# One transformer layer with adaLN, one core: adaLN sums over the free axis, weights laid out in blocks, and five k-passes in the first feed-forward stage

## What is computed

```python
cond = jax.nn.silu(c)                       # 2048 values
mod = cond @ w_ada[l] + b_ada[l]            # 2048 x 18432, nine vectors of 2048
sh1, sc1, gt1, sh2, sc2, gt2, sh3, sc3, gt3 = split(mod, 9)
u = _modulate(_rmsnorm(h, norm1_g[l]), sh1, sc1)          # x * (1 + sc1) + sh1
h = h + 0.5 * gt1 * _swiglu(u, ffn1_w_in[l], ffn1_w_out[l])
u = _modulate(_rmsnorm(h, norm2_g[l]), sh2, sc2)
h = h + gt2 * _hybrid_mixer(u, ...)
u = _modulate(_rmsnorm(h, norm3_g[l]), sh3, sc3)
h = h + 0.5 * gt3 * _swiglu(u, ffn2_w_in[l], ffn2_w_out[l])
return _rmsnorm(h, final_g)
```

## Time and profile before

| | |
|---|---|
| median of 3 runs | 2054.93 us |
| lowest, highest | 2054.68, 3204.81 us |
| span of the profiled execution | 2052.8 us |
| its mean granted TensorE clock | 0.999 |
| TensorE busy | 99% of the span |
| VectorE, ScalarE busy | 85%, 58% |
| moved by DMA | 540.80 MB, mean 263 GB/s |

### The profile page before, as it was taken

One profiled execution on the slowest core, in us unless ns is written; L12 is line 12 of the kernel. 1 busy time (PEld: TensorE's weight loads), 2 busy tenths in 40 slices (PEclk: granted clock), 3 DMA queues, 4 the chain that ended last, 5 costly groups with the idle time before them and its releaser, 6 DMA issues.

```text
span 2052.8 us, 24243 instructions
## 1 busy us (share of the span) xinstructions
PE 2030.3 (99%) x9197; PEld 1674.2 (82%) x9197; DVE 1735.4 (85%) x2038; ACT 1195.1 (58%) x1668; POOL 4.5 (0%) x22
## 2 busy tenths in 40 slices
PE   7999999999999999999999999999999999999998
PEld 6888888888888888888777888888888888888887
DVE  6998998888889898887998898988778777787786
ACT  4667444655346565446545666567775477755764
POOL 0000000000000000000000000000000000000000
PEclk9999999999999999999999999999999999999999
DMA  9998899998999778985666687565565556565554
GB/s 371 387 387 321 328 334 338 343 336 315 327 341 336 269 261 326 334 299 181 218 217 211 230 298 278 204 216 195 186 240 191 202 185 204 206 205 192 177 200 149
DMA packets 249572, 540.80 MB, mean 263 GB/s; under 512 B 11888, under 2 KB 14320, under 8 KB 248688
## 3 DMA queue, kind: packets, MB, share of 16 engines
q1 hardware_dynamic: 248368, 539.11, 74.1%
q10 hardware_dynamic: 1088, 0.15, 0.0%
HBM read 537.10 MB, written 2.11 MB: 263 GB/s over the span
## 4 chain that ended last, share of the span: by engine, by line
PE 94%; DMA 2%; DVE 2%; issue 1%; ACT 0%; SPq 0%; ACTq 0%; DVEq 0%
PE pb L909 13%; PE pb L917 13%; PE pa L909 13%; PE pb L913 13%; PE pa L917 13%; PE pa L913 12%; PE pa L1064 2%; PE pa L1058 2%; PE pa L1061 2%; DMA raw<-in_ffn_w_in_dram 1%; PE pa L1228 1%; PE pb L1219 1%; PE pb L1224 1%; PE pb L1228 1%; PE pa L1219 1%; PE pa L1224 1%
## 5 line engine op out<-in xcount | busy, mean ns | idle before, releaser
L1494 ACT CAST hi<-raw 128x1024 fp32r<-128x1024 f32 (+2 forms) x662 | 682.2, 1035 | 704.8 <-PE pb L917 316.3
L2105 DVE TENSOR_TENSOR lo<-raw,hi 128x1024 fp32r<-128x1024 f32 (+2 forms) x662 | 784.0, 1199 | 230.5 <-ACT hi L1494 228.0
L2205 DVE SCALAR_TENSOR_TENSOR ada_acc<-ada_w,cond,ada_acc 128x1024 f32<-128x1024 f32 (+1 forms) x210 | 236.7, 1127 | 6.3
L909 PE MATMUL pa<-hi,act_hi 128*128 128x512 f32 x816 | 226.4, 394 | 0.0
L909 PE MATMUL pb<-hi,act_hi 128*128 128x512 f32 x816 | 221.0, 393 | 0.0
L917 PE MATMUL pb<-lo,act_hi 128*128 128x512 f32 x816 | 218.2, 389 | 0.0
L917 PE MATMUL pa<-lo,act_hi 128*128 128x512 f32 x800 | 217.8, 389 | 0.0
L913 PE MATMUL pb<-hi,act_lo 128*128 128x512 f32 x800 | 214.0, 389 | 0.0
L913 PE MATMUL pa<-hi,act_lo 128*128 128x512 f32 x736 | 200.3, 389 | 0.0
L917 PEld LDWEIGHTS pb<-lo,act_hi 128*128 128x128 f32 x816 | 153.2, 188 | 32.0
L909 PEld LDWEIGHTS pb<-hi,act_hi 128*128 128x128 f32 x816 | 151.8, 188 | 32.7 <-issue 2.2
(11 more groups left out here) (482 smaller groups left out, 2622.1 us busy)
## 6 DMA issues: line engine op xcount, KB each, us to landing
raw<-in_ffn_w_in_dram SPq DMA_DIRECT2D x155, 1024.0 KB, 5.4
ada_w<-in_w_ada_dram SPq DMA_DIRECT2D x207, 512.0 KB, 6.4
raw<-in_w_in_dram SPq DMA_DIRECT2D x63, 1024.0 KB, 5.3
raw<-in_ffn_w_out_dram SPq DMA_DIRECT2D x60, 1024.0 KB, 5.2
ada_s<-in_w_ada_dram SPq DMA_DIRECT2D x64, 512.0 KB, 11.6
pair<-in_ffn_w_in_dram SPq DMA_DIRECT2D x20, 1024.0 KB, 6.7
raw<-in_ffn_w_out_dram SPq DMA_DIRECT2D x24, 768.0 KB, 4.5
raw<-in_w_out_dram SPq DMA_DIRECT2D x16, 1024.0 KB, 5.1
```

Of the source, the lines that this page charges most:

```text
L909: pe.matmul(bank[:, tt, cols], a_hi[:, k0 + kk, tok], w_hi[:, kk, cols], start=start and kk == 0, stop=False, skip_group_check=on)
L1494: act.copy(hi_of(ph, i, j, half)[:, 0:n, 0:w], raw_of(ph, i, j)[:, 2 * half:2 * half + n, 0:w])\
L2105: dve.tensor_tensor(lo_of(ph, i, j)[:, s, 0:w], raw_of(ph, i, j)[:, s, 0:w], hi_of(ph, i, j, half)[:, 0:n, 0:w].bitcast(F32), ALU.subtract)\
L2205: ins = dve.scalar_tensor_tensor(out=acc, in0=wt, scalar=cond[:, kt:kt + 1], in1=acc, op0=ALU.mult, op1=ALU.add)
```

## The change

**Layout.** The host now hands over every weight matrix in blocks of 512 columns, [block, partition, k-tile, column], so that a partition's part of a chunk is one run of 8 KB in memory; before it was four runs of 2 KB. The chunks of the first stage are laid out in the order of use (`w_first`). x comes token by partition, and once more transposed (`x_t`); parameters come as columns (`cols`).

**adaLN.** `w_ada` is transposed: outputs are on the partitions, k is in the free axis. TensorE spreads `cond` over all partitions once (`cond_rows`, 16 matmuls), and one instruction multiplies a tile with that row and sums it into one column of `macc` (`accum_out`). `mod_sum` adds the two halves and the bias. Folds, flushes and gate sums are gone. The modulation vector lies on the partitions at once; the gate rows, GT1's too now, are stored to DRAM in pieces of 4 bytes and loaded back over all partitions (`store_quarter`, `load_quarter`).

**First stage.** Scale and shift of one k-tile need one tile of 128 x 2048 each (1 MB), so `act_hi` exists k-tile by k-tile. `PASSES` goes through 2, 2, 4, 4 and 4 k-tiles. In a pass two column groups are done first in four double banks (`pa`, `pb`, `px`, `pq`), then the other two in the same banks; ScalarE keeps a bank in `part` and refills it from there (`keep`). `S_AT` gives the units at which VectorE sums the scale and the shift tile of each k-tile. x is not transposed on TensorE: `x_t` is multiplied with the gain and the row of 1/rms. In the opening the first scale tile is loaded between the two halves of x, and summed before the norm.

**adaLN in `ffn1_out0`.** 22 of the 24 tiles lie in its first 11 chunks.

The core of the diff:

```diff
+PASSES = ((0, 1), (2, 3), (4, 5, 6, 7), (8, 9, 10, 11), (12, 13, 14, 15))
...
-    ada_plan("ffn1_out0", [2, 1, 2, 1] * 4)
+    ada_plan("ffn1_out0", [2] * 11 + [1, 1, 0, 0, 0])
...
+    NEW = {kt: min(u for u in range(64) if kt in [b[0] for b in first_unit_of(u)[2]]) for kt in range(KD)}
+    S_AT = {0: (0, 0), 1: (1, 2), 2: (6, 7), 3: (8, 9), 4: (13, 14), 5: (16, 17), 6: (18, 19), 7: (20, 21),
+            8: (27, 28), 9: (29, 30), 10: (32, 33), 11: (34, 35), 12: (43, 44), 13: (45, 46), 14: (48, 49), 15: (50, 51)}
+    XT_PIECES = ((0, 2), (2, 4), (4, 8), (8, 16))
...
+            def store_quarter(q):
+
+                sp.wait_ge(mod_ok, mod_count(GT1, q))
+                sp.dma_start(gate_rows[0:1, q * NC:(q + 1) * NC].rearrange("a (k p) -> p (a k)", p=P),
+                             mod[:, GT1 * KD + 4 * q:GT1 * KD + 4 * q + 4], allow_slow_non_contiguous=True)\
+                    .then_inc(gt1_out, 16)
...
-            sp.dma_start(h[:, :, :], x_tok).then_inc(x_in, 16)
-            for k in range(8):
-                load_start(k)
...
+            sp.dma_start(c_in[:, :], c).then_inc(c_ok, 16)
+            for tt in range(TT):
+                sp.dma_start(h[:, tt, :], x[:, tt, :]).then_inc(x_in[tt], 16)
+                if tt == 0:
+                    load_start(0, (SC1,))
+            load_x_t(0)
+            load_start(0, (SH1,))
+            loaded = 1
+            for pos in range(32):
+                ahead = pos + (pos >= 12)
+                while loaded < KD and NEW[loaded] // 2 <= ahead:
+                    for piece, (k0, _) in enumerate(XT_PIECES):
+                        if k0 == loaded:
+                            load_x_t(piece)
+                    load_start(loaded)
+                    loaded += 1
+                load(plan["ffn1_in0"], 0, pos, w_first[pos], 4)
                 load_ada(plan["ffn1_in0"].c0 + pos)
...
+                cond_rows()
+                keep_busy(8)
+                rstd_row()
+                keep_busy(24)
+                pe.wait_ge(cond_row_ok, 4)
+                pe.wait_ge(rs_ok, 1)
+                for u in range(64):
+                    if u == 57:
+                        pe.wait_ge(pa_free, 2)
+                        transposes(0)
+                    if u in (60, 63):
+                        nb = (u - 57) // 3
+                        pe.wait_ge(nat_lo, 2 * nb)
+                        transposes(nb)
+                    first_unit(ph, u)
...
+                def keep(p, g, ab, after):
+
+                    bank = ((px, pq) if second_set(p, g) else (pa, pb))[ab]
+                    act.wait_ge(unit_used, after + 1)
+                    act.copy(part[:, g, ab, :, :], bank[:, :, :]).then_inc(part_ok if p > 0 else bank_ok, 1)
+                    if p > 0:
+
+                        other = (g + 2) % 4
+                        act.wait_ge(bank_ok, 4)
+                        act.wait_ge(part_ok, 4 * (p - 1) + 2 * (g % 2) + ab + 1)
+                        act.copy(bank[:, :, :], part[:, other, ab, :, :]).then_inc(bank_ok, 1)
...
+                for u in range(64):
+                    split(ph, 0, u // 2, u % 2, 2)
+                    for kt in range(KD):
+                        if NEW[kt] == u:
+                            first_hi(kt)
+                    for job in todo.get(u, ()):
+                        keep(*job)
...
+            def start_tile(kt, m):
+
+                k = 2 * kt + (m == SH1)
+                dve.wait_ge(ada_s_in[k % S_RING], 16 * (k // S_RING + 1))
+                wt = ada_s[:, k % S_RING, :]
+                dve.scalar_tensor_tensor(out=wt, in0=wt, scalar=1.0, in1=cond_row[:, :], op0=ALU.mult, op1=ALU.mult,
+                                         accum_out=macc[:, 0, m * KD + kt:m * KD + kt + 1]).then_inc(s_dve, 1)
...
+                for u in range(64):
+                    for kt in range(KD):
+                        if S_AT[kt][0] == u and kt > 0:
+                            start_tile(kt, SC1)
+                        if S_AT[kt][1] == u:
+                            start_tile(kt, SH1)
+                            start_mod(kt)
+                    for kt in range(KD):
+                        if NEW[kt] == u:
+                            start_lo(kt)
...
                     split(ph, 0, u // 2, u % 2, 2)
```

More of the change, by code:

```diff
@@ L123, in build, with tile_col @@
     SH1, SC1, GT1, SH2, SC2, GT2, SH3, SC3, GT3 = range(9)
[L124 to L140, removed]
+    HALF_ROWS = [(GT1, q) for q in range(4)] + [(m, half) for m in (SH2, SC2, GT2, SH3, SC3, GT3) for half in (0, 1)]
+    ROWS_OUT = (GT1, GT2, GT3)
+    ROW_TILES = [8 if m == GT1 else 16 for m, _ in HALF_ROWS]
+    TILES = [(row, sub) for row in range(len(HALF_ROWS)) for sub in range(ROW_TILES[row])]
+    def tile_col(t):
+        row, sub = TILES[t]
+        m, part_ = HALF_ROWS[row]
+        return m * KD + part_ * (ROW_TILES[row] // 2) + sub // 2, sub % 2
     n_tiles = {}
@@ L208, in s_used, with mod_after, mod_count @@
-    def s_used(q, n):
-        on_dve = sum(kt not in ON_PE[x // KD] for x in range(KD * q + n) for kt in (x % KD,))
-        return on_dve, KD * q + n - on_dve
+    MODS = [(GT1, q) for q in range(4)] + [(m, 1) for m in (SH2, SC2, GT2, SH3, SC3, GT3)]
+    def mod_after(t):
+        row, sub = TILES[t]
+        return HALF_ROWS[row] if sub == ROW_TILES[row] - 1 and HALF_ROWS[row] in MODS else None
+    def mod_count(m, part_=1):
+        return MODS.index((m, part_)) + 1
+    S_RING = 4
+    FIRST = first_chunks()
@@ L214, in build, with second_set, bank_at @@
+    def second_set(p, g):
+        return g % 2 == 1 and not (p == LAST and g == 3)
+    def bank_at(p, g, ab):
+        return 4 * p + (2 * (g - 2) if p == LAST else 2 * (g % 2)) + ab + 1
     PIECES = [(g, (0,)) for g in range(4)] + [(g, (1,)) for g in range(4)] + [(g, (0, 1)) for g in range(4, 8)]
@@ L1225, in first_unit @@
                               start=False, stop=False, skip_group_check=True)
                 pe.wait_ge(lo_done, u + 1)
-                for kk, tt, tok in places:
-                    mm = pe.matmul(bank[:, tt, :], act_hi[:, k0 + kk, tok], w_lo[:, 2 * half + kk, 0:NC],
-                                   start=False, stop=half == 1 and kk == 1, skip_group_check=True)
+                for m, tt, tok in places:
+                    mm = pe.matmul(bank(m)[:, tt, :], act_hi[:, blocks[m][0], tok], w_lo[:, s0 + m, 0:NC],
+                                   start=False, stop=True, skip_group_check=True)
@@ L1532, in in_body @@
                     split(ph, i, j, half, n)
-                    if ph is plan["ffn1_in1"] and first and n_ == 0:
-                        gate_round(3)
                     if first and mid:
@@ L2494, in body @@
                         split(ph, i, j, half, n)
-                        if name == "ffn1_in1" and first and n_ == 1:
-                            gate_rest(3)
                         if first and mid:
```

893 lines of the change are left out of this document (303 added, 590 removed).

## The result

The changed kernel takes 2068.61 us (median of 4, 2067.85 to 2071.29) where the kernel before takes 2054.84. The ratio is 1.0069, with a 95% interval of 1.0054 to 1.0084. It lies inside 2%, but the interval is clear of 1, and the time is outside the range of 2037 to 2061 that was forecast. Two single executions ran far slower (one of the kernel before, 3204.81 us; one of e11_runs_order, 2526.46 us at a granted clock of 0.752), and the ratios are taken without them.

What follows compares the result with a forecast made beforehand. TensorE, busy 99%, was taken as the bound, with VectorE next. Span 2052.8 - 0.4 (first stage) - 4.0 (rest) = 2048.4, plus 2.1 to the median, 2050.5 us; forecast's own range 2045 to 2056, 8 in 10 for 2037 to 2061.

Steps and rivals of the forecast that it cites:

- Opening: Start of the first stage: unit 0 at about 20.6 us, 15.6 us earlier than before, and unit 2 at 28.3.
- The tile: VectorE's 2048-wide scale or shift sum in the first stage: taken as 2.27 us, between 2.2 and 2.7.
- Rival C: Slower kernel because the summing tile costs more than 2.27 us; at 2.7 us, 2061.7 us in all; chance 0.15.
- Stalls (a) to (c): First stage, units 16 to 21, 28 to 35, 43 to 51: VectorE's tile bursts stall TensorE 6.3, 5.8 and 4.7 us.
- ScalarE's eight copies: Behind units 10 and 11, keeping and refilling four banks at 1.0 us a copy cuts VectorE's lead to 1.4 us.
- VectorE, not the transfers, takes it: First stage: VectorE gives back nearly all the opening's gain; the stage ends at 217.4 us against 217.75.
- rival B: Long runs bring no faster transfer: 387 GB/s instead of 417, plus 4 us, 2054.5 us; chance 0.13.
- The rest, minus 4.0: Behind the first stage: removing TensorE's gate sums saves 2.0 us and its folds 2.0 us; bounds 2.5 and 5.
- The doubled tiles: `ffn1_out0`, 22 tiles in 11 chunks: VectorE's 21.7 us per block just fits TensorE's 21.8, nothing to spare.
- The gate row "cost nothing": GT1's trip through DRAM in `ffn1_out0`: loaded some 5.4 us into the stage, some 18 us to spare, no cost.
- which sign would overturn the step: A wait of VectorE on the gate row in `ffn1_out0` or `ffn1_in1` would overturn costing it at nothing.
- the forecast's span of 2048.4: Whole kernel: the span before, 2052.8 us, less 0.4 for the first stage and 4.0 for the rest.

Runs made afterwards that it cites:

- e11_runs_order: e10_long_runs with another order in the first stage, of SyncE's tile transfers and of the units where VectorE sums them; 2039.65 us, ratio to before 0.9924.
- e3_tile_half: The changed kernel with half of each first-stage scale and shift sum left out, the transfers kept; 2061.97 us.
- e8_gate_pe_keeps: e1_gate_pe with ScalarE's first-stage bank copies spread, one pair per unit; 2056.75 us.
- e12_tile_half_both: The changed kernel with half of each first-stage scale and shift tile left out, in the sum and in the transfer; 2045.58 us.
- e13_order_again: The kernel of e11_runs_order run once more for another trace; 2040.59 us, ratio to before 0.9928.
- e10_long_runs: The changed kernel with gate rows stored in runs, 16-byte pieces for GT1 and 64-byte for GT2 and GT3; 2054.01 us, ratio to before 0.9996.
- e1_gate_pe: The changed kernel with the GT1 row spread by TensorE and copied by VectorE, instead of going through DRAM; 2056.69 us.
- e5_gate_pe_store: e1_gate_pe with the four quarter stores in 4-byte pieces kept, nothing waiting for them or reading them; 2066.88 us.
- e7_before_pieces: The kernel before with four stores of 512 4-byte pieces added, which nothing reads or waits for; 2069.69 us against 2055.29.

## Why the prediction was wrong, step by step

**Opening: right.** Unit 0 starts at 20.72 us (forecast 20.6), unit 2 at 29.00 (28.3).

**The tile: right.** A 2048-wide sum is followed after 2.21 us, with 2.27 taken. Rival C falls with it.

```profile
21.83 2.29 DVE L1995 SCALAR_TENSOR_TENSOR ada_s<-ada_s,cond_row 128x2048 f32<-128x2048 f32 x1
24.04 0.08 DVE L1995 DVE_READ_ACCUMULATOR ada_s<-ada_s,cond_row 128x1 f32 x1
```

**Stalls (a) to (c): right in place and size, the engine half right, one reason wrong.** TensorE's gaps in units 16 to 21, 28 to 35 and 43 to 51, from the start of one matmul to the next less the usual, add up to 5.2, 5.3 and 4.9 us (6.3, 5.8 and 4.7 were said). Against 2.72 us for each unit, which is how the forecast counted, the three stretches lose 6.3, 6.1 and 5.8. The stage ends at 219.5 us (217.4). They are nearly all waits for VectorE, and with half of each sum gone most of them go (e3_tile_half). But other waits, for the cast, take their place at units 34 and 50, 7.8 us of them, and only 4.8 us are won. So VectorE's bursts are one cause, and not shown to be the whole. ScalarE's eight copies, which were to cut the lead to 1.4 us, are worth 0.6 us at the stage's end (e8_gate_pe_keeps).

**"VectorE, not the transfers, takes it": half right.** Transfers run at 420 GB/s where they run, as said, so rival B as it was put falls. But they are a second limit right behind VectorE (e3_tile_half against e12_tile_half_both), and neither was full, since the transfers' share fell to 0.78 and 0.74 in between. The sum took the stalls as the price of the bursts. They were the price of one order, and in e13_order_again, with all the work in it, TensorE has no wait left in those units.

**The rest, minus 4.0: right.** It is read where the pieces are gone: e10_long_runs goes from +1.7 to -2.1 us between the start of `ffn1_out0` and the end, 3.9 us. That bears out the sum of the gate sums and folds; their shares were not measured. The doubled tiles do just fit.

**The gate row "cost nothing": the step that failed.** The sum asked when quarter 0 is wanted and found some 18 us to spare. That figure left out the store's own landing: stored at 225.26 us, it landed 12.5 us later, so the load was issued 18.3 us into the stage and not 5.4, landed at 243.45 us, and the row was used at 253.18. Some 10 us were left, and VectorE waits only once, 0.3 us for quarter 3. So the step's result held with a wrong working, and it answered the wrong question. The text said which sign would overturn the step, a wait of VectorE on the row, and all that came of it is this 0.3 us. What came is what the step left out, the price that a transfer's shape puts on all other transfers. Each quarter is stored as 512 pieces of 4 bytes. Together with GT2's and GT3's stores, which had become 2048 pieces of 4 bytes each, that costs 14.6 us here (15.4 of span, 2066.1 against 2050.7 of e10_long_runs). The quarters' stores alone cost 14.4 us in the kernel before and 10.2 on top of e1_gate_pe. With all of it out, the forecast's span of 2048.4 stands beside 2050.7, and 2.1 of the difference is the first stage's later end; that was the fastest of the kernel's executions, and its median of 2054.01 lies 3.5 above the forecast's 2050.5. The warning was to be had ahead: the kernel before has no store of a row in 4-byte pieces, only GT2's and GT3's in pieces of 128 bytes, so it was an operation without a row, and it should have had a price from both sides and a rival.

A rule that spoke against it was also at hand. The Trainium skill, "DMA: Bandwidth & Descriptors", section "Specifications", says that below 512 bytes a DMA engine reads, modifies and writes. The traces agree that small pieces can be dear, but not with that limit: 16-byte and 64-byte pieces are below it as well and cost nothing that these runs show.

## What to carry to other kernels

Cost a new DMA by what it does to the transfers behind it, not only by when its data is wanted; a store whose innermost run is one 4-byte element should be laid out in runs first, by turning the weight's rows if nothing else. When an engine stalls in bursts while it and the transfers each stand idle at other times, write down the order of both queues and move the work before calling either a limit.

## What the runs showed that I had not expected

- A 2 KB store in 4-byte pieces slows the transfers of all 16 DMA engines for some 7 us: 176 GB/s and 80 GB/s behind it, at a mean DMA share of 1.1. The pieces themselves are written down with 9 ns each. The same bytes in 16-byte pieces: 339 GB/s. What in the DMA engines makes the packets behind the pieces slow is not shown.
- A store may take long to land and cost nothing: with 16-byte pieces it lands after 9.1 us in the median (15.2 with 4-byte ones), and the kernel is as fast as without it.
- After a wait of 4.66 us TensorE's next eight matmuls took 3.5 us instead of 1.8, at a granted clock of 0.57 from 273 to 277 us. The same came 1 us after a wait of 2.24 us, and in e5_gate_pe_store right after waits of 2.84 and 2.48. It didn't come after 2.49 us in the changed kernel's opening, after 2.07 in e7_before_pieces, or after 1.47 and less.
- Why four short stores cost more in the kernel before (14.4 us) than on e1_gate_pe (10.2) stays open.
